# An expert's u and v as one 8 KB row and one gather, in a two-layer decoder trunk with product-key experts

## The reference

```
def peer(h, wq, keys, u_tab, v_tab):
    ...
        q = (xc @ wq).reshape(c, PEER_HEADS, 2, PEER_QDIM // 2)
        sc = jnp.einsum('thpd,hpkd->thpk', q, keys, preferred_element_type=jnp.float32)
        top_v, top_i = lax.top_k(sc, PEER_TOPK)
        ...
        ids = jnp.take_along_axis(cand_id, best_pos, axis=-1)
        gate = jax.nn.softmax(best_v, axis=-1)
        ug = u_tab[ids]
        act = jax.nn.gelu(jnp.einsum('td,thkd->thk', xc, ug, preferred_element_type=jnp.float32)) * gate
        vg = v_tab[ids]
        return jnp.einsum('thk,thkd->td', act.astype(vg.dtype), vg)
```

## Time and profile before

| | |
|---|---|
| median of 3 runs | 1743.39 us (1742.62 to 1750.01) |
| profiled execution, first to last instruction | 1741.3 us |
| PE / DVE / ACT / POOL busy | 1460.4 / 1130.7 / 458.2 / 1098.4 us |
| DMA | 634.77 MB, 365 GB/s over the span |
| gathers | 1024, 538.00 MB in the queue of POOL |

### The profile page before, as it was taken

How to read it: one execution, slowest core, us unless ns; L and a number is a source line. 1 busy time by engine, 2 the same in 40 slices (tenths; PEclk the granted TensorE clock), 3 DMA queues, 4 the chain that set the end, 5 groups by cost and what they waited for, 6 DMA issues and landing times.

```text
span 1741.3 us, 15891 instructions
## 1 busy us (share of the span) xinstructions
PE 1460.4 (84%) x4754; PEld 780.2 (45%) x4754; DVE 1130.7 (65%) x2791; ACT 458.2 (26%) x1118; POOL 1098.4 (63%) x1037
## 2 busy tenths in 40 slices
PE   7886979799987898888989699789989777777777
PEld 4655435454564444444465345355456333222232
DVE  6865998564466787774467698665546876563443
ACT  3522244242211223342121224334122122121111
POOL 1014658677747567776776667777674766656664
PEclk9998989999989999998999899899989988888888
DMA  9378999999999999999999999999999999999997
GB/s 362 121 278 302 332 384 338 355 325 410 387 379 375 411 413 406 408 361 394 407 404 410 353 413 409 348 348 356 393 405 357 366 362 374 373 367 366 370 361 301
DMA packets 176177, 634.77 MB, mean 365 GB/s; under 512 B 17713, under 2 KB 18353, under 8 KB 173534
## 3 DMA queue, kind: packets, MB, share of 16 engines
q0 software_dynamic: 147872, 538.00, 80.9%
q1 hardware_dynamic: 28222, 95.77, 14.1%
HBM read 631.06 MB, written 2.64 MB: 364 GB/s over the span
## 4 chain that ended last, share of the span: by engine, by line
PE 37%; POOL 17%; DVE 17%; issue 13%; DMA 9%; another core or an unknown queue 5%; ACT 1%; SPq 0%; DVEq 0%; POOLq 0%; ACTq 0%
PE ps L1520 21%; POOL ring_u L1557 9%; POOL ring_v L1565 8%; DVE ring_u L1176 6%; PE ps L1487 6%; DMA ring_u<-table_u,ids 5%; PE ps L1297 4%; DMA ring_v<-table_v,ids 3%; PE ps L1465 2%; PE ps L1503 1%; DVE W L954 1%; DVE W L1149 1%; DVE W L1151 1%; DVE W L1152 1%
## 5 line engine op out<-in xcount | busy, mean ns | idle before, releaser
L1520 PE MATMUL ps<-ring_v,diag 128*128 128x512 f32 x2048 | 983.5, 636 | 194.8 <-issue 124.2
L1565 POOL DMA_INDIRECT ring_v<-table_v,ids x512 | 534.7, 1044 | 345.1 <-PE ps L1520 175.1
L1520 PEld LDWEIGHTS ps<-ring_v,diag 128*128 128x128 f32 x2048 | 408.0, 204 | 721.6 <-issue 679.8
L1557 POOL DMA_INDIRECT ring_u<-table_u,ids x512 | 558.3, 1091 | 265.9 <-issue 151.4
L1176 DVE CUSTOM_DVE_ANT_0 ring_u<-ring_u,h 128x1024 f32<-128x1024 f32 x384 | 455.5, 1223 | 154.0 <-DMA ring_u<-table_u,ids 77.1
L707 ACT ACTIVATE acts<-dots,small 128x4 f32<-128x4 f32 x128 | 38.0, 297 | 907.8 <-DVE dots L1176 475.0
L1176 DVE CUSTOM_DVE_ANT_0 ring_u<-ring_u,ps 128x1024 f32<-128x1024 f32 x128 | 154.4, 1221 | 137.3 <-DMA ring_u<-table_u,ids 113.1
L718 ACT ACTIVATE diag<-cst,weights 128x128 f32<-128x128 f32 x512 | 163.5, 390 | 29.9 <-DVE weights L1185 19.0
L1487 PE MATMUL ps<-hT,W 128*128 128x128 f32 x960 | 122.1, 286 | 19.4 <-issue 19.2
L1487 PEld LDWEIGHTS ps<-hT,W 128*128 128x128 f32 x960 | 117.1, 201 | 25.2 <-issue 25.2
L1297 PE MATMUL ps<-W,hT 128*128 128x512 f32 (+2 forms) x256 | 95.2, 527 | 2.7 <-DVE hT L828 2.7
(11 more groups left out here) (296 smaller groups left out, 1136.0 us busy)
## 6 DMA issues: line engine op xcount, KB each, us to landing
W<-peer_wq SPq DMA_DIRECT2D x13, 2048.0 KB
W<-w_in SPq DMA_DIRECT2D x16, 1282.0 KB
W<-w_out SPq DMA_DIRECT2D x8, 2048.0 KB
ring_u<-table_u,ids POOLq DMA_INDIRECT x512
ring_v<-table_v,ids POOLq DMA_INDIRECT x512
W<-w_in SPq DMA_DIRECT2D x8, 898.0 KB
W<-w_in SPq DMA_DIRECT2D x4, 1024.0 KB, 11.4
ring_u<-w_in SPq DMA_DIRECT2D x2, 1544.0 KB, 18.3
```

Source lines behind the costliest of these rows:

```text
L1520: mm = pe.matmul(ps[:, c, :], diag[:, s, :], ring_v[:, s, c * 512:(c + 1) * 512], start=(k == 0), stop=(k == SLOTS - 1), skip_group_check= ...
L1557: gp.indirect_dma_start(ring_u[:, k % RING, :], None, table_u, bass.IndirectOffsetOnAxis(ap=ids[:, b, k:k + 1], axis=0)).then_inc(u_in[k % ...
L1565: gp.indirect_dma_start(ring_v[:, k % RING, :], None, table_v, bass.IndirectOffsetOnAxis(ap=ids[:, b, k:k + 1], axis=0)).then_inc(v_in[k % ...
```

## The change

Four things change together.

1. `table_u` and `table_v` become one table, `table_uv`, with u and v of an expert side by side: one row of 8 KB. This is done on the host, outside the kernel's time. One gather brings both, so there are 512 gathers of 128 x 8 KB in place of 1024 of 128 x 4 KB.
2. The two rings of eight places of 4 KB become one ring of ten places of 8 KB (`RING = 10`). A place is taken again when the matmuls of its v are done. The dots, gelu results, weights and diagonals keep eight places (`HELD`). Each dot waits for its pair (`pair_in`), so for both rows.
3. Room for this comes from the memory that holds the DMA descriptors of GpSimd (`dynamic_dma_scratch_size=4096`; it was the default of 16384 bytes a partition), from `small` (768 to 416 numbers) and from the buffer `glu`.
4. `glu_w` is loaded in every pass into room that is free at that time, so four times instead of two. `wq_early` moves to places 8 and 9 of the ring, where no other weights lie, and loses its wait.

```
-RING = 2 * RING_G
+HELD = 2 * RING_G
+RING = 10
...
-        ring_u = sb("ring_u", [P, RING, D])
-        ring_v = sb("ring_v", [P, RING, D])
+        ring = sb("ring", [P, RING, 2 * D])
...
+        def glu_at(n):
+
+            c0 = 7168 if n == 0 else 2048
+            return (T if n else pool)[:, c0:c0 + 2 * GW].rearrange("p (k n) -> p k n", k=2)
...
                 if n == 0:
-                    sp.wait_ge(z_ps, 4)
+                    sp.dma_start(wq_early, wq_quarters[1]).then_inc(wq_early_in, 16)
                     sp.wait_ge(lines_out, 16)
-                    sp.dma_start(wq_early, wq_quarters[1]).then_inc(wq_early_in, 16)
+                else:
+                    sp.wait_ge(logit_ps, 4 * n + 4)
+                sp.dma_start(glu_at(n), glu_w[layer].rearrange("(k p) n -> p k n", p=P)).then_inc(glu_load, 16)
...
                 for j in range(RING_G):
-                    s = g * RING_G + j
-                    v.wait_ge(u_in[s], 16 * (m // 2 + 1))
+                    s, r = g * RING_G + j, (RING_G * m + j) % RING
+                    v.wait_ge(pair_in[r], 16 * ((RING_G * m + j) // RING + 1))
...
                     for k in range(RING_G * i, RING_G * (i + 1)):
-                        if m >= 2:
-                            gp.wait_ge(dots_done, SLOTS * n + k - RING + 1)
-                        gp.indirect_dma_start(ring_u[:, k % RING, :], None, table_u,
-                                              bass.IndirectOffsetOnAxis(ap=ids[:, b, k:k + 1], axis=0)).then_inc(u_in[k % RING], 16)
-                    if m == 0:
-                        gp.wait_ge(z_ps, 8)
-                        gp.wait_ge(s5_out, 16 * (DEPTH - 1))
-                    for k in range(RING_G * i, RING_G * (i + 1)):
-                        if m >= 2:
-                            gp.wait_ge(v_used, SLOTS * n + k - RING + 1)
-                        gp.indirect_dma_start(ring_v[:, k % RING, :], None, table_v,
-                                              bass.IndirectOffsetOnAxis(ap=ids[:, b, k:k + 1], axis=0)).then_inc(v_in[k % RING], 16)
+                        t = SLOTS * n + k
+                        if t >= RING:
+                            gp.wait_ge(v_used, t - RING + 1)
+                        elif t == 0:
+                            gp.wait_ge(z_ps, 4)
+                        elif t == 4:
+                            gp.wait_ge(z_ps, 8)
+                            gp.wait_ge(s5_out, 16 * (DEPTH - 1))
+                        elif t == 8:
+                            gp.wait_ge(qT_ps, 2)
+                        gp.indirect_dma_start(ring[:, t % RING, :], None, table_uv,
+                                              bass.IndirectOffsetOnAxis(ap=ids[:, b, k:k + 1], axis=0)).then_inc(pair_in[t % RING], 16)
...
-    nc = bacc.Bacc("TRN2", target_bir_lowering=False, num_devices=1)
+    nc = bacc.Bacc("TRN2", target_bir_lowering=False, num_devices=1, dynamic_dma_scratch_size=4096)
```

More of the change, by code:

```diff
@@ L219, in plan_steps, with trunk @@
     return plan
-def trunk(nc, x_in, w_in, w_out, row_in, gain_ffn, s5_in, glu_w, peer_wq, keys_t, table_u, table_v,
+def trunk(nc, x_in, w_in, w_out, row_in, gain_ffn, s5_in, glu_w, peer_wq, keys_t, table_uv,
           rel_bias, const_in, bucket_in, out):
@@ L243, in trunk @@
         s5t = sb("s5t", [P, 3072])
-        glu = sb("glu", [P, 2, GW])
-        small = sb("small", [P, 768])
+        small = sb("small", [P, 416])
         mags = sb("mags", [P, DEPTH, NJ])
@@ L248, in trunk @@
         gates = sb("gates", [P, NB, SLOTS])
-        dots = sb("dots", [P, RING])
-        acts = sb("acts", [P, RING])
-        weights = sb("weights", [P, RING])
-        diag = sb("diag", [P, RING, P])
+        dots = sb("dots", [P, HELD])
+        acts = sb("acts", [P, HELD])
+        weights = sb("weights", [P, HELD])
+        diag = sb("diag", [P, HELD, P])
         key_rows = sb("key_rows", [P, HP * NK])
@@ L259, in trunk @@
         wq_slots = [W[:, 2560 + 4096 * i:6656 + 4096 * i].rearrange("p (k n) -> p k n", k=KC) for i in range(2)]
-        wq_early = ring_u[:, 4:8, :].rearrange("p a d -> p (a d)").rearrange("p (k n) -> p k n", k=KC)
+        ring_u, ring_v = ring[:, :, 0:D], ring[:, :, D:2 * D]
+        pool = ring[:, :, :].rearrange("p a d -> p (a d)")
+        wq_early = pool[:, 16384:20480].rearrange("p (k n) -> p k n", k=KC)
         def wq_at(n, i):
@@ L267, in trunk @@
         first_at = [t.rearrange("p (k n) -> p k n", k=KC) for t in (
[L268 to L269 removed]
+            W[:, 8192:16384], pool[:, 0:KC * (FIRST_CUTS[2] - FIRST_CUTS[1])],
+            pool[:, 8192:8192 + KC * (FIRST_CUTS[3] - FIRST_CUTS[2])])]
         T = W[:, 0:8192]
@@ L328, in trunk @@
         s5_tabled, s5_out, out_stored = sem("s5_tabled"), sem("s5_out"), sem("out_stored")
-        u_in = [sem(f"u_in{i}") for i in range(RING)]
-        v_in = [sem(f"v_in{i}") for i in range(RING)]
+        pair_in = [sem(f"pair_in{i}") for i in range(RING)]
         dots_done, gelu_done, weights_done, diag_ready, v_used = (
@@ L445, in _ @@
             sp.dma_start(s5p[1], s5_in[1]).then_inc(s5_in_done[1], 16)
-            sp.dma_start(glu[:, :, :], glu_w[0].rearrange("(k p) n -> p k n", p=P)).then_inc(glu_load, 16)
             def load_chunk(n, k):
@@ L465, in _ @@
                         sp.dma_start(s5t[:, :], s5_dram[layer - 1]).then_inc(s5_load, 16)
-                        sp.dma_start(glu[:, :, :], glu_w[layer].rearrange("(k p) n -> p k n", p=P)).then_inc(glu_load, 16)
                     for k in range(WIN_SLOTS, KC):
@@ L1436, in glu_out @@
                 pe.wait_ge(gT_ready, n + 1)
-                pe.wait_ge(glu_load, 16 * (n // NB + 1))
+                pe.wait_ge(glu_load, 16 * (n + 1))
                 for j in range(2):
-                    mm = pe.matmul(ps[:, 6, 0:256], gT[:, j * P:(j + 1) * P], glu[:, j, :], start=(j == 0), stop=(j == 1))
+                    mm = pe.matmul(ps[:, 6, 0:256], gT[:, j * P:(j + 1) * P], glu_at(n)[:, j, :], start=(j == 0), stop=(j == 1))
                 mm.then_inc(glu_ps, 1)
```

33 lines of the change are left out of this document (13 added, 20 removed).

## The result

The changed kernel takes 1631.47 us (median of 4 runs, 1631.40 to 1632.62). The kernel before, beside it on the same chip, takes 1746.70 us (4 runs, 1742.62 to 1751.09). One thing has to be known for all that follows. In five later sessions, on five chips (numbers 10, 4, 3, 2 and 6), the kernel before took 1650 to 1653 us. On four of them the changed kernel ran beside it and took 1627 to 1631 us, a ratio of 0.984 to 0.988. So some 24 of the first 115 us belong to the change wherever it ran, and the other 91, about four fifths, to the kernel before in the first comparison.

A forecast was written before the change was run, and what follows sets the result against it. It took POOL's gather issue as the bound in the last pass and some mixed stretches, PE or DMA in others. From a 1741.3 us span, minus 32 (mixed) and 36 (last pass), plus 2.1 to the median: 1675 us; range 1640 to 1733.

The forecast's parts named there:

- POOL sets the pace: Last pass and some mixed stretches: POOL's 1.24 to 1.41 us per 4 KB gather barely beats or lags DMA's 1.28 us.
- From below its cost to POOL is that of one now: Lower end for an 8 KB gather on POOL, issue included: 1.24 to 1.41 us, the end the prediction took.
- The last pass, 36 us: Gathers alone at 415 GB/s: 317 us, 43 saved, less 5 for latency at the end and 2 for the start.
- The mixed stretches, 32 us: From 250 to 1377 us: DMA savings at 415 GB/s, capped by PE's idle time, 53 us together, of which 60% taken.
- no more than half of PE's idle time: Cap on what each mixed stretch could save through faster DMA; the stretches together gave 53 us.
- I book no gain: Before 250 us: first pairs ready as before and DMA not full in three slices, so nothing counted.
- I book the ring at nothing: Ring of ten pairs: a stall's start costs 5 us less, its end about 5 more; range -5 to +5 each.
- some 6 us of slack: Tour of the ring takes 25 us; after holding places and 6.7 us from issue to landing, about 6 us remain.
- The late dots, free but for 5 us at the end: Dots waiting for v start about 5 us later; DVE has room, so the latency is paid once, at kernel end.
- places are held too long: Rival, 1.2 in 10: mixing steps exceed the slack in mixed stretches, DMA runs dry, late dots are paid: 1782 us.
- The weights, taken at nothing: `peer_wq` quarters beside 8 KB gathers: a full ring throttles gathers, leaving weights about 140 GB/s, 15 us, so no cost.
- The scratch, `glu_w` twice more: Quartered descriptor memory taken at nothing, at worst about 2 us per pair; two extra `glu_w` loads, 1.3 us of DMA.

## Why the prediction came out as it did, step by step

**POOL sets the pace.** Right in the mixed stretches, and sharper than it was put. POOL's time for a pair against the 2.49 us of its data decides: 2.35 us cost 0 to 3 us, 2.67 cost 75 us in all (1702.54 to 1627.14). "From below its cost to POOL is that of one now": the gather of twice the row cost 1.13 us on average, 0.94 in the last pass. For the last pass it was wrong. On chip 4 the kernel before moves 409 GB/s there at a share of 1.03, the rate of gathers alone in the earlier trace rows. There DMA is the limit, and POOL's 2.48 us a pair fit inside it. That it moved 365 GB/s on the first chip goes with the late signals there; this is read from the traces and was not tested.

**The last pass, 36 us.** On the first chip 43. The number was met by luck: 33 of the 43 us are the difference of the kernel before between the first chip and chip 4 (361.7 and 328.8), which the sum did not know of. The 9 us left, 2.7%, are near the ratio of the two rates (409 to 421). The rate was put at 415 GB/s and was 421. The Trainium skill ("DMA: Bandwidth & Descriptors", "Why small descriptors are slow (HBM only)") with its 3 cycles a packet makes 409 an estimated 414; the rows here show 421, so from 4 KB to 8 KB the rate rose by 3% and not by 1.1%, and the measurement decides.

**The mixed stretches, 32 us.** This is the step that failed: "no more than half of PE's idle time", of that 60%, because "many of PE's gaps there are waits between PE and DVE that no DMA ends; the earlier trace rows show one of 15 us". On the first chip 69 us came back, more even than the 53 before the cut to 60%: 59 us in the stretches that were summed and 10 us before 250 us, where "I book no gain". The 15 us wait was no property of the program: the matmul that it waited for had ended 14 us before. A look at PE's row at 1089.37 would have shown it, beside "remote" as the releaser. On the other chips 20 us came back in the first three passes, so there the same step was too high. Both terms together, 68 us, stand against 115 on the first chip and some 24 on the others.

**"I book the ring at nothing."** Right with ten places: +0.2 to 0.3% for holding them, with the other small parts of the change in it. But only with ten. With nine places the change is hardly faster than before (0.9941), with eight slower. The "some 6 us of slack" was an over-estimate: two places are 5.0 us of data, and losing them costs 3.6% (1.0216 against some 0.986), 58 us.

**The late dots, free but for 5 us at the end.** Wrong where it was measured: 17.9 us, with two gathers of 4 KB rows in turn. The rival "places are held too long" had the mechanism ("the 5 us by which dots now come later are paid on the path"). It is real at some 18 us there, and the one gather gains 48 against it. What the late dots cost in the changed kernel itself, where POOL has time to spare, no run shows.

**The weights, taken at nothing, "up to 8 us for each of three passes".** Wrong: with `peer_wq` in time the changed kernel is 12 to 16 us faster (1615.08 against 1627 to 1631 on other chips; 8 to 15 by the ratios), with `w_out` too 18, against a bound of 24. The argument that a full ring throttles the gathers failed. In the window above q0 moved 5.18 MB in 16 us, 324 GB/s, where 265 was assumed, and the weights got 89 and not 140 GB/s. The rate by turns, 80 GB/s, had stood in the text and was talked away.

**The scratch, `glu_w` twice more.** The first at nothing: right. The second was not tried by itself; it is part of the 6.7 us of the ring.

So the errors had opposite signs. The ring, the late dots and the late weights cost up to 40 us (6.7 + 17.9 + 16) that were booked at 5. And about 90 of the 115 us on the first chip (115.2 less the 24 of the other chips) were a delay of the kernel before that the change all but ended, of which the sum took in only a part, because it read some of that delay as waits of the program and some as POOL's pace. A gain was right on every chip, but its size met neither: too low where the delay was, too high elsewhere. The cause of the delay stays open.

## What to carry to other kernels

Compare an issuing engine's time for one transfer with the time of its data. Here a saving below it was worth nothing, and above it nearly the whole excess was paid on every transfer. Before larger pieces go into one DMA queue, look at the pieces of the others: with one packet each in turn, as here, the share of the small ones falls with the ratio of the sizes, and a host layout with long rows gave it back. Where a wait is charged to the program, look up the end of what it waited for; if that is long past, the wait need not be the program's, and the kernel should be timed on a second chip first.

## What the runs showed of the hardware

Gathers of 128 rows of 8 KB ran at 421 GB/s where those of 4 KB ran at 409, and cost POOL the same 0.94 us each in the last pass. The DMA share passes 1.00 with gathers alone (1.01 and 1.03), so without two queues too. The Trainium skill ("DMA: Bandwidth & Descriptors", "Queues, rings and completion order") says that an engine takes turns between queue rows by packets of typically 9 to 17 descriptors. The counts of the trace, 1095 to 1006 and 711 to 712, agree with turns in that they are near one for one in the profile's packets; how many descriptors make a turn they do not show. On the first chip the kernel before was 5.7 to 5.9% slower than on five others, with matmul completions noticed up to 14 us late; the cause stays open.
